# Moving the indexer's score units one slot later in a hand-written step order, on a hybrid attention kernel

## The reference: what is computed

```python
def project(x, norm_g, w_in, ...):
    h = rms_norm(x, norm_g)
    p = h @ w_in                       # 1024 -> 2884 columns
    qa, ka, va, ga, qb, kb, vb, gb, qi, ki, wi = split(p)
    # qa, ka, qb, kb: RMS norm per head of 64; qi: 4 indexer heads of 64; ki: 64; wi: 4 weights
...
def dsa_attend(q, qi, wi, k_all, v_all, ki_all, t_pos, topk, rel_bias):
    r = relu(einsum('bqhe,ble->bqhl', qi, ki_all))
    score = einsum('bqhl,bqh->bql', r, wi)
    score = where(admissible, score, -inf)
    _, idx = top_k(score, topk)        # 256 keys per query
    ...                                # attention over these keys alone
```

## Time and profile before

| what | value |
|---|---|
| median of 3 runs | 5989.77 us |
| lowest, highest | 5989.61, 5996.18 us |
| time of the profiled execution | 5994.54 us |
| its span, first to last instruction | 5992.7 us |
| mean granted clock of TensorE | 0.888 |
| last instruction of VectorE's last search (L968) starts | 2724.5 us |

### The profile page before, as it was taken

One profiled execution on the slowest core, in us unless ns is written; L12 is line 12 of the kernel. 1 busy time (PEld: TensorE's weight loads), 2 busy tenths in 40 slices (PEclk: granted clock), 3 DMA queues, 4 the chain that ended last, 5 costly groups with the idle time before them and its releaser, 6 DMA issues. The chain is left out here.

```text
span 5992.7 us, 72577 instructions
## 1 busy us (share of the span) xinstructions
PE 4587.5 (77%) x24809; PEld 2921.5 (49%) x24809; DVE 3637.4 (61%) x5854; ACT 3295.2 (55%) x6314; POOL 1709.1 (29%) x1408
## 2 busy tenths in 40 slices
PE   7978787777666666500888888899999899899378
PEld 3434344433333333300666666677777677444145
DVE  1265688888988898894666666566565665011400
ACT  1557788887887888741555555555555555000211
POOL 1334556667567757600211100000000000000000
PEclk9988888888877777755899999999999999999778
DMA  4111111100000000005221111101010100333140
GB/s 116 42 42 37 35 40 38 36 33 29 33 27 31 26 33 23 24 18 103 71 60 48 44 45 38 36 29 37 27 35 25 37 24 8 135 116 109 26 119 4
DMA packets 215223, 275.40 MB, mean 46 GB/s; under 512 B 54176, under 2 KB 146048, under 8 KB 214848
## 3 DMA queue, kind: packets, MB, share of 16 engines
q1 hardware_dynamic: 214864, 270.76, 14.9%
HBM read 163.35 MB, written 108.39 MB: 45 GB/s over the span
## 5 line engine op out<-in xcount | busy, mean ns | idle before, releaser
L527 PE MATMUL bank<-w,x 128*128 128x512 f32 (+1 forms) x3168 | 1402.0, 598 | 15.3 <-DVE w L866 12.1
L968 DVE TENSOR_SCALAR_CACHE_REDUCE ties<-score,cand 128x512 bf16<-128x512 f32 (+14 forms) x480 | 1254.0, 2613 | 139.8 <-POOL score L844 123.1
L733 ACT ACTIVATE act_junk<-score,a_cand,a_sign 128x384 int8<-128x384 f32 (+14 forms) x450 | 990.3, 2201 | 15.0
L527 PEld LDWEIGHTS bank<-w,x 128*128 128x128 f32 x3168 | 638.0, 206 | 667.5 <-issue 612.4
L1490 ACT ACTIVATE pT<-bank 128x512 f32<-128x512 f32 (+2 forms) x704 | 371.1, 527 | 902.6 <-PE bank L1387 791.3
L1466 ACT ACTIVATE row<-row,top 128x1024 f32<-128x1024 f32 (+7 forms) x896 | 759.6, 849 | 91.3 <-DVE top L1547 75.4
L1387 PE MATMUL bank<-ident,row 128*128 128x128 f32 x4728 | 682.0, 280 | 166.1 <-DVE pT L1613 76.8
L543 PE MATMUL bank<-kiT,qi 128*128 128x512 f32 (+3 forms) x1136 | 397.8, 496 | 536.6 <-DVE kiT L886 311.6
L1557 DVE CUSTOM_DVE_ANT_0 row<-bank,mask 128x1024 f32<-128x1024 f32 (+7 forms) x576 | 567.7, 1017 | 332.8 <-PE bank L1369 331.4
L1369 PE MATMUL bank<-kT,q_part 128*128 128x512 f32 (+3 forms) x2560 | 639.3, 380 | 113.8 <-DVE part L1557 113.3
L1387 PEld LDWEIGHTS bank<-ident,row 128*128 128x128 f32 x4728 | 524.1, 141 | 283.1 <-DVE pT L1613 99.2
(11 more groups left out here) (219 smaller groups left out, 4594.8 us busy)
## 6 DMA issues: line engine op xcount, KB each, us to landing
gates<-ring SPq DMA_DIRECT2D x66, 256.0 KB, 2.0
qk_t<-ring SPq DMA_DIRECT2D x66, 256.0 KB, 2.0
gate<-gates SPq DMA_DIRECT2D x33, 512.0 KB, 3.4
x<-in_x_prompt SPq DMA_DIRECT2D x32, 512.0 KB, 3.6
q_raw<-qk_t SPq DMA_DIRECT2D x64, 256.0 KB, 4.2
mixed<-mixT SPq DMA_DIRECT2D x64, 256.0 KB, 2.0
mix_in<-mixed SPq DMA_DIRECT2D x32, 512.0 KB, 4.2
x_in<-in_x_prompt SPq DMA_DIRECT2D x32, 512.0 KB, 3.8
```

The costliest lines, as they stand in the source:

```text
L527: ins = pe.matmul(p_bank[n % 2][:, 0:n1 - n0], x[t % 2][:, c * P:(c + 1) * P], w[:, c, n0:n1], start=(c == 0), stop=(c == KC - 1))
L733: tick(act.activation(junk, row, ACT.Sign, bias=c, scale=back, accum_out=a_sum[:, :]))
L968: n = tick(dve.tensor_scalar(ties[:, 0:width], row, c.bitcast(F32), 0.0, ALU.is_ge, ALU.add, accum_out=counts[:, i:i + 1]))
```

## The change

```diff
 def unit_slot(u, j):
 
-    return j * 8 // len(units(u))
+    return 1 + j * 8 // len(units(u))
...
     for a in range(first, TILES, 2):
-        clock = max(clock, us_at(a + 1, 8.7))
+        clock = max(clock, us_at(a + 1, 9.6))
...
                         if slot == 11 and t < TILES:
-                            yield us_at(t, slot)
+                            yield us_at(t, slot - 0.5)
                             split_q(t)
                             split_k(t)
```

## The result

The changed kernel takes 6084.53 us (median of 5 runs, 6075.16 to 6086.07), the kernel before 5993.37 us in the same measurement. The ratio is 1.015 with a 95% interval of 1.0136 to 1.0164, so the change costs 91 us. The profiled execution of the changed kernel took 6075.16 us with a span of 6073.3 us, 80.6 us over the span of before; it was the fastest of the five, so what is read from the two profiles is some 10 us less than the medians differ by.

What follows compares the result with a forecast made beforehand. No engine is full; a two-step loop of waits from score row to score row bounds stage one. Loops from step 16 to 32 +45, earlier loops -4: +41 us, 6031 us; own range 6002 to 6075, with rivals 5965 to 6090.

Steps and rivals of the forecast that it cites:

- The loop: Stage one, two steps: score row, VectorE's tests and splits, TensorE's unit 0, eight units, next row; 223.2 us in the late loop.
- Part 1: VectorE's order from score row to odd step's split: +4.9 us in the late loop, +3.1 us in that of step 22.
- The first term: Even step's split in the late loop: ends 12.0 us behind the score row instead of 20.2, counted as -8.2 us.
- R: Moment the score row of an odd tile is ready, always in an even step; the late loop's even split was forecast 12.0 us later.
- The second: Three more VectorE tests between the two splits from step 16 on: +13.1 us in the late loop.
- Part 2: Unit 0 behind key transposes and first projection: 8.3 us later start, 5.5 us of GpSimd waits back, +2.8 us in the late loop.
- The bound of that part: Unit 0 behind the first projection: with none of GpSimd's waits returned, at most +8.3 us a loop.
- Part 4: Loops before step 16, where ScalarE sets when the even split comes: -4 us together, with ends at -30 and +10.
- The clock: First projection on TensorE after an idle stretch: 8.7 us, not the 14 us of a whole projection at 1.2 GHz.
- The faster one: Rival: early loops decide, each 5 to 7 us shorter, -32 us for five, late loops level; about 5960 us, chance 0.15.
- The level one: Rival: late loops cost half (+20) as all GpSimd waits return, early loops give 20; 5990 us, chance 0.13.
- The much slower one: Rival: ScalarE's copy comes no earlier and none of the projection returns, +124 us; 6114 us, chance 0.12.

Runs made afterwards that it cites:

- e4: Changed kernel with unit 0's relus on ScalarE due at their slot, not 0.6 slot later, removing the test before them: 6079.38 us.
- e6: Kernel before with TensorE's units alone moved one slot later, ScalarE and GpSimd in their old slots: 6044.84 us.
- e9: Changed kernel with seven of eight partial products of the first projection left out from step 3 on, values wrong: 5981.25 us.
- e13: Kernel before with seven of eight partial products of the first projection left out from step 3 on, values wrong: 5947.82 us.
- e11: Changed kernel with an odd step's split put ahead of the choice for the even tile: 5987.01 us.
- e1: Kernel before with only the units moved one slot later, search start and splits as before: 6040.96 us.
- e3: Changed kernel with unit 0 alone put back ahead of the first projection on all engines: 6093.04 us.
- e5: Kernel before with units one slot later on ScalarE and GpSimd only, TensorE's units in their old slots: 6212.04 us.
- e8: Kernel before with the whole change for tiles and steps up to 13 only: 5984.84 us.
- e14: Changed kernel with odd splits ahead of the choice for the even tile and even splits behind test 1 of the new search: 5984.08 us.

## Why the prediction was right in direction and wrong in size

The loop was the right one. The loss came through a later odd split and a longer way from it to the row, as forecast; TensorE's wait moved as forecast; VectorE waits 3.7 to 9.3 us for the copy in steps 16 to 28 (forecast 3 to 8); everything behind stage one kept its length within 5 us. The full range, 5965 to 6090, holds 6084.5, but the forecast's own range ended at 6075: it said +41 and the chip +91. In the two profiles the last row came 85.5 us later where the sum had 41: 15 us of the difference are part one, 33 part two, and 4 less the early loops.

*Part 1 of the prediction (VectorE's splits).* Forecast +4.9 us in the late loop and +3.1 in that of step 22; measured +6.7 (134.1 to 140.8) and +5.0. The first term is right: the split ended at R + 12.2 (forecast 12.0). The second was too small. Between the splits there are 14.8 us more than before, not 13.1. The operation of a test took what I had priced; what grew is the last of its small instructions. VectorE's small two-input instruction in the stretch between the splits, first before, then changed:

```profile
L975 DVE SCALAR_TENSOR_TENSOR cand<-flag,cand 128x1 int32<-128x1 int32 x19 | 6.1, 322 | 0.7
```

```profile
L975 DVE SCALAR_TENSOR_TENSOR cand<-flag,cand 128x1 int32<-128x1 int32 x22 | 8.6, 392 | 0.8
```

2.5 us more for three more of them, where three undisturbed take 0.5 us: the other 2.0 us cover the missing 1.7. Every one of these that took over 0.2 us, in either stretch, ran beside an instruction of GpSimd. Over the eight loops part one is 39 us where the forecast's seven at about 4, less 4, make 24.

*Part 2 (unit 0 behind the first projection).* This is the term that failed. I took 8.3 us for the later start and 5.5 us back from GpSimd's idle time, +2.8 us a loop; measured +4.1 to +9.3, 54.5 us in eight loops where I had 22. Both of its halves were mis-sized. GpSimd started 74 us later in eight loops where 8.3 a loop makes 66, and 21 us of its idle time came back where 5.5 a loop makes 44.

In the late loop that I worked out, the start was wrong and the return right. The start is 12.3 us later, not 8.3: I had read the planner's places as if the evacuation and unit 0's relu stood together, while in steps 22 to 30 a whole test lies between them. GpSimd's waits on relu inside step 30 fell from 7.4 us to 1.7; 12.3 less 5.7 is the measured 6.4 within 0.2 us:

```profile
POOL score L835 <- ACT relu L664: 1.7, 1, 1.7
```

In step 24, too, 5.7 us came back. In the other six steps the return was too small. In steps 18 and 20 the start moved by only 4 us, since the first relu had stood 5.3 us behind the split before, and the idle time did not shrink (+1.6 and -0.5 us); in steps 22, 26, 28 and 32 it gave 0.9 to 4.0 us. Nor are the two halves independent, as my sum had them: in e4, with the test gone, the waits reappeared in front of unit 1. In step 30 of e4:

```profile
POOL score L835 <- ACT relu L664: 5.5, 2, 3.8
```

What the runs put in place of the term is a chain: the split, the projection, unit 0, and then GpSimd's work on all units, 77 us in step 30, of which the change takes nothing away. The projection's 8 to 9 us on TensorE begin only with the split, since the key transposes in front of it need the split's bank; so the chain starts later by the projection, and in five steps by a test besides, and it makes up only what it had waited. In TensorE's order the last unit stands behind one more projection where there are five to seven units, but behind as many as before in steps 30 and 32, and there the row is 6.4 and 9.3 us late all the same. e6 (TensorE's order alone, +53), e9 against e13 (59 against 17 us of part two) and e11 (the projection covered, 98 us given back) show this from three sides. Within part two the shares of TensorE's projection and of ScalarE's order stay open: e6 has 33 of the 51 us that e1 has in the late loops, e3 and e4 show that ScalarE's place for unit 1 has a share, and e5, which was to give it, created a wait of its own.

*The bound of that part was too narrow for the same reason*: I put 8.3 us as the most a loop could lose here, and three loops lost 8.5 to 9.3. The start alone was 8.8 to 12.3 us later in six of the eight loops.

*Part 4 (before step 16)* forecast -4, measured -8; e8 shows that it would have lasted. *The clock*: a first projection behind an odd split took 8.20 to 9.46 us in steps 16 to 32, near the 8.74 us of the earlier trace rows that I took; over the one of 8.20 us the granted clock was 0.86. By the Trainium skill (TensorE: Matmul & The Clock Gate, Part 1) an idle array runs at 1.2 GHz, and the estimate for a whole projection at that level was 14 us; the trace shows that none of these ran at it throughout.

*The rivals.* The faster one asked that VectorE's wait for the copy in steps 8 to 14 grow by under 2 us; it grew by 6.0, 2.5, 2.1 and 5.6 us. The level one asked that all of GpSimd's waits return; of the 57 us of waits on relu in the eight loops 21 did, and the early loops gave 8 us and not 20. The much slower one asked that the copy come no earlier and that nothing return: the copy came 5 us earlier in the late loop (R + 11.1), and the 21 us were returned. Its 18.3 us a loop were too many as my 6.7 were too few; measured are 11.7.

## What to carry to other kernels

When an order written by hand moves a piece behind another, look at what releases the other. Here the projection needed a buffer that the same late event frees, so it filled no wait and put off the start of a chain of eight units; the same order costs nothing once that event comes before the next engine is ready (e11). A due time taken from a plan moves pieces by whole tests: count the tests on the loop between releasing and released piece, and ask if the piece can run there at all. And the end of such a chain moves by its start, its work and its idle time together: idle time that comes back counts against the later start, but only as much as there was in each loop, and where one unit alone moves, the wait comes back in front of the next (e3, e4).

## What the runs showed of the hardware

GpSimd's weighings and adds slow down beside VectorE's scan and two-input instructions. In the changed kernel, step 28:

```profile
2118.54 8.04 DVE L897 TENSOR_TENSOR_SCAN score<-ties 128x3328 f32<-128x3328 bf16 x1
2119.59 7.82 POOL L837 TENSOR_TENSOR relu<-relu,weight 128x512 f32<-128x512 f32 x1
...
2126.62 4.28 DVE L902 SCALAR_TENSOR_TENSOR ties<-score,pick,ties 128x3328 bf16<-128x3328 f32 x1
2127.50 4.52 POOL L840 TENSOR_TENSOR score<-score,relu 128x512 f32<-128x512 f32 x1
```

The weighing that took 1.04 us elsewhere took 7.82 us, and ended just behind the scan. The scan has `ties` as both of its inputs. Summed over a step, GpSimd's weighings and adds take 8 to 19 us longer than undisturbed ones in the even steps from 18 on, before and after the change alike. The Trainium skill has the rule (SBUF — State Buffer, SBUF: two separate sides): VectorE with two inputs in SBUF and a GpSimd instruction that reads it exclude each other for the whole instruction. The trace agrees, with these four rows: both of GpSimd's instructions end about 1 us behind VectorE's. It holds in the other direction for the 0.16 us instruction above, which took 0.39 us on average. It was not tried to move the scan out of the units' way.

The fastest kernels whose work is complete are e14 and e8, 0.13% and 0.15% under the kernel before, with intervals of 0.9977 to 0.9996 and 0.9976 to 0.9993: 5984.08 and 5984.84 us. Such differences are small, and each rests on 11 executions against 15.
